# Rotary partners by a lane shuffle on VectorE instead of permutation matmuls, in a two-block transformer kernel

## The chip, the core and the metric

The kernel runs on one core of a Trainium2 chip. The metric is the device time of one execution, in microseconds (us). TensorE (PE in the profile, with PEld for its weight loads) multiplies matrices, VectorE (DVE), ScalarE (ACT) and GpSimd (POOL) work elementwise, and SyncE (SP) issues most of the DMAs. The engines run side by side and meet at semaphores. SBUF is the working memory, and PSUM has eight banks into which TensorE writes.

## The reference: two blocks over 256 tokens of width 1024

Everything is float32. The part that the change touches is the rotation of queries and keys in either block; the rest is named so that the stages can be followed.

```
# block 1: 8 heads of neighbourhood attention, 12 heads of dilated attention
h = rms_norm(x, norm_mix);  proj = h @ w_in
qd = partial_rotary(rms_norm(qd), pos)      # first 16 of each head's 64 channels
kd = partial_rotary(rms_norm(kd), pos)
    x1, x2 = xr[..., :8], xr[..., 8:16]
    rot = concat([x1*cos - x2*sin, x2*cos + x1*sin])
x = x + (sigmoid(gate_na) * (out_na @ w_branch_na)
         + sigmoid(gate_dil) * (out_dil @ w_branch_dil)) @ w_out
x = x + peer_ffn(rms_norm(x))               # 16384 experts, 8 heads x top 16
x = x + sigmoid(rms_norm(x) @ w_ple_gate) * (p @ w_ple)
# block 2: pooling branch and 4 differential-attention heads
q = apply_rope(q, cos, sin);  k = apply_rope(k, cos, sin)   # all 64 channels
    t1, t2 = split(t, 2)
    rope = concat([t1*cos - t2*sin, t1*sin + t2*cos])
x = x + mix @ w_o;  x = x + (silu(gate) * val) @ w_down;  out = rmsnorm(x)
```

## The kernel before

Activations stand with their channels on the 128 partitions and the 256 tokens along the free axis, so a chunk of 128 channels is a 128x256 tile and holds two heads of 64. All weights come in slots of 128x1024 (512 KB), loaded into `RAW` by SyncE. Each slot is split into a high part, rounded to fp32r by ScalarE (`split`, line 1101), and a low part, the difference, by VectorE or GpSimd (lines 1554 and 2273; `low_on_dve` says which). TensorE then makes three fp32r products for one weight block (`mm3`): high by high, high by low, low by high. There are three split buffers: slot n is split when TensorE has used slot n - 3, and loaded when the low part of slot n - 4 is made.

Each engine has its own program, written out in order. Generators set that order: `first_steps` for the first block's mixing part, `peer_steps` for the experts, `second_steps` for the second block's. Every step name stands in all five programs, and each program does its own part of it. Keys in `up` and `at` are semaphore counts; an engine waits in its own order only.

In the first block, step `ld n` computes chunk n of the 12 dilated query and key chunks (24 matmuls); `ev n` is ScalarE's part: copy the chunk with its gain into `qkd` (line 1144) and square it into one of four buffers `sqr` (line 1147). Step `dq i` rotates chunk i one step later. TensorE multiplies `qkd` by the constant 128x128 matrix `permd` in full float32, which exchanges channels 0 to 7 with 8 to 15 of each head with the sign (the result is the tile `rot` in PSUM), and `qk_sum` sums the squares of the chunk's two heads with two small matmuls per chunk. VectorE makes chunk x cos (line 1703), waits for TensorE's `rot`, multiplies it by sin (line 1708), and adds (line 1710). Steps `sc`, `tp` and `pv` between them are the scores, transposes and value products of the neighbourhood attention.

In the second block, `lin n` computes chunk n of 8; ScalarE copies it raw to `qk2` (`raw2`, line 1424); step `rp n` has TensorE multiply it by `permr`, which exchanges the 32-channel halves of each head, and VectorE makes the same three operations (lines 2143, 2147, 2149). The cos and sin tiles (`cosr`, `sinr`) already hold the norm's factor by token. Step `sc i` needs chunks 2i and 2i + 1 rotated; its scores are masked and their maxima taken by VectorE (lines 2156 to 2161), exponentiated by ScalarE (`exp`), combined by VectorE (`soft`).

The expert part has 128 slots `u` (projections; from slot 48 on each gives hidden values with a high and a low sum, added at line 2033) and 128 slots `v` (the way back). ScalarE applies gelu to slot u's values (line 1310), and VectorE multiplies in the gates (`gated_u`, line 1954), which frees the PSUM bank. Slot `v 0` begins the eight output sums in eight banks in the order 0, 1, 4, 5, 7, 6, 2, 3; the last of them needs the bank of slot u 127.

## Time and profile before

| | us |
|---|---|
| median of 3 runs | 1322.82 (1321.11 to 1323.88) |
| the profiled execution, its own time | 1317.93 |
| its span in the trace | 1315.8 |
| TensorE busy | 1302.9 |
| VectorE / ScalarE / GpSimd busy | 1013.6 / 827.2 / 520.3 |

The profiled execution is one run apart from the three timed ones. The span is what the trace covers; 2.1 us of the profiled execution's time lie around it. In a row of the timeline, the first number is the start in us from the span's start, the second how long the group lasts, then engine, line, operation, output<-inputs, shapes and the count of instructions; a bracket gives the idle time before it and what ended it. A matmul in full float32 stands as two records, an fp32r matmul as one. Matmuls are pipelined: each record's length is longer than the distance to the next one's start.

### The profile page before, as it was taken

The page shows a single profiled execution, that of the slowest core. Times are in us where ns is not written, and L with a number is a line of the kernel's source. Part 1 is how long each engine was busy: PE and PEld are TensorE (multiplying, and loading weights), DVE is VectorE, ACT ScalarE, POOL GpSimd, SP SyncE. Part 2 cuts the span into 40 slices and gives each one's busy share as a digit, 9 for nine tenths or more (in the row PEclk, how much of TensorE's full clock was granted, in tenths as well). Part 3 has the DMA queues.
Part 4 walks back from the last instruction along what each step waited for, and adds up shares of the span by engine and source line. Part 5 has one row for each costly group of instructions (what it writes and reads, how often), then busy time and mean ns, then how long its engine had stood idle before and what let it go on. Part 6 is the DMA issues. An engine that isn't in the chain of part 4 may idle for free.

```text
span 1315.8 us, 24814 instructions
## 1 busy us (share of the span) xinstructions
PE 1302.9 (99%) x9818; PEld 1257.0 (96%) x9818; DVE 1013.6 (77%) x1845; ACT 827.2 (63%) x1679; POOL 520.3 (40%) x252
## 2 busy tenths in 40 slices
PE   9999999999999999999999999999999999999998
PEld 9999899999999999999999999999999999999997
DVE  4483645859999888899978798998868845899943
ACT  5564646545455888888865566555566666666653
POOL 3745567678901000000024444324205463784442
PEclk9999999999999999999999999999999999999999
DMA  8433445445656554454579999999865543556552
GB/s 304 136 112 129 129 129 189 164 165 182 202 182 204 193 174 162 163 173 163 162 248 328 356 346 332 334 331 328 305 209 164 176 129 134 185 171 193 185 191 97
DMA packets 74299, 268.35 MB, mean 204 GB/s; under 512 B 8253, under 2 KB 8637, under 8 KB 74185
## 3 DMA queue, kind: packets, MB, share of 16 engines
q1 hardware_dynamic: 64968, 233.22, 52.5%
q0 software_dynamic: 9216, 33.56, 6.9%
q8 instruction: 78, 1.28, 0.4%
q14 instruction: 37, 0.30, 0.1%
HBM read 265.70 MB, written 1.05 MB: 203 GB/s over the span
## 4 chain that ended last, share of the span: by engine, by line
PE 83%; DVE 10%; POOL 4%; ACT 1%; DMA 1%; issue 1%; SPq 0%; DVEq 0%; ACTq 0%
PE PS L620 82%; POOL SPL L2273 2%; POOL HF L2332 1%; ACT SPL L1101 1%; DMA RAW<-in_ev 1%; DVE ixu L1844 1%; DVE Ssc L1838 1%; DVE ixu L1835 1%; PE PS L763 1%; DVE SPL L1554 1%; DMA RAW<-in_dense 1%; DVE bias L1633 0%; POOL HF L2330 0%; DVE top L1841 0%; DVE top L1832 0%
## 5 line engine op out<-in xcount | busy, mean ns | idle before, releaser
L1101 ACT ACTIVATE SPL<-RAW 128x1024 fp32r<-128x1024 f32 x429 | 453.7, 1059 | 363.0 <-PE PS L620 343.4
L620 PE MATMUL PS<-HS,SPL 128*128 128x224 f32 (+2 forms) x3968 | 531.4, 292 | 0.9 <-DVE SPL L1554 0.7
L620 PEld LDWEIGHTS PS<-HS,SPL 128*128 128x128 f32 x3968 | 502.5, 189 | 12.4 <-issue 1.7
L2273 POOL TENSOR_TENSOR SPL<-RAW,SPL 128x1024 fp32r<-128x1024 f32 x149 | 361.6, 2432 | 259.6 <-ACT SPL L1101 259.4
L1554 DVE TENSOR_TENSOR SPL<-RAW,SPL 128x1024 fp32r<-128x1024 f32 x280 | 345.3, 1235 | 142.6 <-ACT SPL L1101 140.3
L620 PE MATMUL PS<-asp,SPL 128*128 128x448 f32 (+1 forms) x2048 | 321.9, 319 | 1.6 <-DVE GB L1954 1.3
L620 PEld LDWEIGHTS PS<-asp,SPL 128*128 128x128 f32 x2048 | 307.5, 190 | 15.6 <-DVE GB L1954 1.6
L2303 POOL DMA_INDIRECT rows<-in_er,RS x16 | 27.9, 1743 | 281.4 <-PE PS L620 248.0
L620 PE MATMUL PS<-HXb,SPL 128*128 128x256 f32 x720 | 89.3, 284 | 0.7 <-issue 0.5
L620 PEld LDWEIGHTS PS<-HXb,SPL 128*128 128x128 f32 x720 | 87.4, 188 | 1.3 <-issue 1.0
L1317 ACT ACTIVATE oh<-oh,T3f 128x128 f32<-128x128 f32 x224 | 71.4, 404 | 0.0
L1934 DVE TENSOR_TENSOR oh<-CC,T3f 128x1024 f32<-128x1024 f32 x56 | 68.3, 1220 | 0.1
L2303 POOL DMA_INDIRECT urow<-in_er,RS x16 | 28.8, 1798 | 86.1 <-DVE RS L1946 59.1
L620 PE MATMUL PS<-actT,SPL 128*128 128x256 f32 x528 | 62.7, 281 | 0.0
L620 PEld LDWEIGHTS PS<-actT,SPL 128*128 128x128 f32 x528 | 62.6, 188 | 0.0
L620 PE MATMUL PS<-oh 128*128 128x128 f32 x448 | 60.1, 277 | 0.1
L620 PEld LDWEIGHTS PS<-oh 128*128 128x128 f32 x448 | 54.2, 191 | 2.0 <-ACT oh L1317 0.2
L1557 DVE TENSOR_TENSOR asp<-GB,asp 128x224 fp32r<-128x224 f32 x128 | 49.5, 387 | 1.7 <-ACT asp L1356 1.7
L1356 ACT ACTIVATE asp<-GB 128x224 fp32r<-128x224 f32 x128 | 47.8, 373 | 0.0
L2306 POOL DMA_INDIRECT rows<-in_ev,RS x16 | 28.7, 1796 | 47.3 <-DVE rows L2060 47.0
L620 PE MATMUL PS<-HXa,SPL 128*128 128x256 f32 x384 | 46.9, 282 | 0.5 <-POOL SPL L2273 0.5
L2306 POOL DMA_INDIRECT vrow<-in_ev,RS x16 | 26.8, 1676 | 50.3 <-DVE rows L2060 47.5
(296 smaller groups left out, 1525.3 us busy)
## 6 DMA issues: line engine op xcount, KB each, us to landing
RAW<-in_dense SPq DMA_DIRECT2D x176, 512.0 KB, 3.6
RAW<-in_eu SPq DMA_DIRECT2D x128, 512.0 KB, 3.5
RAW<-in_ev SPq DMA_DIRECT2D x128, 512.0 KB, 6.0
bias<-in_nab SPq DMA_DIRECT2D x2, 768.0 KB, 8.3
XT<-in_xT SPq DMA_DIRECT2D x4, 256.0 KB, 6.6
out_y<-HF SPq DMA_DIRECT2D x4, 256.0 KB, 2.2
c<-in_c SPq DMA_DIRECT2D x1, 960.0 KB, 8.9
c<-in_c SPq DMA_DIRECT2D x1, 512.0 KB, 4.7
```

The source lines that it names most:

```text
L620: return e.matmul(out, l, r, start=start, stop=stop, skip_group_check=skip)
L763: t = e.transpose(ps[:, j, a * 128:a * 128 + 128], probs_of(tag, i)[:, a * 256 * chunks + c * 256 + j * 128: a * 256 * chunks + c * 256 + ...
L1101: e.activation(spl(n)[0], raw(n), ACT.Copy).then_inc(*up("act_high", ("hi", n)))
L1317: q = e.activation(oh[m % 2][:, 1, j, :], oh[m % 2][:, 1, j, :], ACT.Copy, scale=T3f[:, 2, 4 * m + j:4 * m + j + 1])
L1356: e.activation(asp[i % 4][:, 0:W], GB[:, i, :], ACT.Copy).then_inc(*up("act_part", ("ahi", i)))
L1554: e.tensor_tensor(lo, raw(n), hi.bitcast(f32), ALU.subtract).then_inc(*up("dve_low", ("lo", n)))
L1557: return e.tensor_tensor(lo, x, hi.bitcast(f32), ALU.subtract).then_inc(*up("dve_part", *keys))
L1835: e.max_index(it[:, 0:8], vt[:, 0:8], v).then_inc(*up("dve_top", ("where1", k)))
L1934: e.tensor_tensor(oh[m % 2], con("iota").unsqueeze(1).unsqueeze(1).to_broadcast([128, 2, 4, 128]), T3f[:, 0:2, 4 * m:4 * m + 4].unsqueeze( ...
L2273: e.tensor_tensor(lo, raw(n), hi.bitcast(f32), ALU.subtract).then_inc(*up("pool_low", ("lo", n)))
L2303: e.indirect_dma_start(urow[j % 2], None, A["er"], rows_).then_inc(*up(f"urow{j % 2}", ("urow", j), by=16))
L2306: e.indirect_dma_start(vrow[j % 2], None, A["ev"].rearrange("a b c -> (a b) c"), rows_).then_inc(*up(f"vrow{j % 2}", ("vrow", j), by=16))
```

## The change

1. The matrices `permd` and `permr` and their 12 + 8 matmuls go. In step `dq`, VectorE's `stream_shuffle` moves the partitions of `qkd` in place within each group of 32 (`PARTNER_8`); the product with sin is then in SBUF, with the sign in the table. In step `rp`, the shuffle reads the chunk from PSUM and writes `qk2` (`PARTNER_16`), and ScalarE's `raw2` copies go. So that a half's partner lies within 32 partitions, the weights' columns of the second block's queries and keys are ordered anew by the host, the table of frequencies too.
2. `qk_sum` of two neighbouring chunks is done together, in the `dq` step of the odd one.
3. At the last `u` slot, ScalarE's `gelu(127)` and VectorE's `gated_u(127)` stand ahead of the split made in that slot. Before, they stood at the start of step `v 0`, behind it.

```diff
-for _n, _w in (("ident", 128), ("iota", 128), ("permd", 128), ("permr", 128), ("fold", TG)):
+for _n, _w in (("ident", 128), ("iota", 128), ("fold", TG)):
...
+PARTNER_8 = [*range(8, 16), *range(8), *range(16, 32)]
+PARTNER_16 = [*range(16, 32), *range(16)]
...
                 elif what == "dq":
-                    ps = take("scr1", "rot", i)
-                    w.wait_ge(*at("qksq", 8 + i))
-                    mm(ps[:, 0:256], con("permd"), qkd[:, i, :]).then_inc(*up("pe_rotate", ("full", "rot", i)))
-                    qk_sum(8 + i)
+                    if i % 2:
+                        qk_sum(7 + i)
+                        qk_sum(8 + i)
...
-                elif what == "rp":
-                    ps = take("scr3", "rp", i)
-                    w.wait_ge(*at("raw2", i))
-                    mm(ps[:, 0:256], con("permr"), qk2[:, i, :]).then_inc(*up("pe_rotate", ("full", "rp", i)))
...
                         if i > ROUTED:
                             gelu(i - 1)
+                    if i == NE - 1:
+                        gelu(i)
                     if i >= SUMS_FIRST:
                         split(cur[0] - 1 + NSPL)
...
                 elif what == "v":
-                    if i == 0:
-                        gelu(NE - 1)
...
-            def raw2(n):
-                w.wait_ge(*at("full", "qk2", n))
-                e.activation(qk2[:, n, :], psum("qk2", n)[:, 0:256], ACT.Copy).then_inc(*up("act_copy", ("raw2", n)))
...
-                    ps = psum("rot", i)[:, 0:256]
-                    w.wait_ge(*at("full", "rot", i))
-                    e.tensor_tensor(ps, ps, c1v["sind"], ALU.mult).then_inc(*up("dve_rotate", ("sined", i)))
+                    o = qkd[:, i, :]
+                    e.stream_shuffle(o, o, PARTNER_8).then_inc(*up("dve_rotate", ("swapped", i)))
+                    w.wait_ge(*at("swapped", i))
+                    e.tensor_tensor(o, o, c1v["sind"], ALU.mult).then_inc(*up("dve_rotate", ("sined", i)))
                     w.wait_ge(*at("sined", i))
-                    e.tensor_tensor(qkd[:, i, :], ps, rotm[i % 2],
-                                    ALU.add).then_inc(*up("dve_rotate", ("rotated", i), ("ev", "rot", i)))
+                    e.tensor_tensor(o, o, rotm[i % 2], ALU.add).then_inc(*up("dve_rotate", ("rotated", i)))
...
+                    if i == NE - 1:
+                        gated_u(i)
                     if i >= SUMS_FIRST:
                         split(cur[0] - 1 + NSPL)
                 elif what == "v":
-                    if i == 0:
-                        gated_u(NE - 1)
...
                 elif what == "rp":
-                    w.wait_ge(*at("raw2", i))
+                    o, ps = qk2[:, i, :], psum("qk2", i)[:, 0:256]
+                    w.wait_ge(*at("full", "qk2", i))
+                    e.stream_shuffle(o, ps, PARTNER_16).then_inc(*up("dve_rotate", ("swapped2", i)))
                     w.wait_ge(*at("turn2", 1))
-                    e.tensor_tensor(rm[i % 2], psum("qk2", i)[:, 0:256], cosr, ALU.mult).then_inc(
+                    e.tensor_tensor(rm[i % 2], ps, cosr, ALU.mult).then_inc(
                         *up("dve_rotate", ("cosed2", i), ("ev", "qk2", i)))
-                    ps = psum("rp", i)[:, 0:256]
-                    w.wait_ge(*at("full", "rp", i))
-                    e.tensor_tensor(ps, ps, sinr, ALU.mult).then_inc(*up("dve_rotate", ("sined2", i)))
+                    w.wait_ge(*at("swapped2", i))
+                    e.tensor_tensor(o, o, sinr, ALU.mult).then_inc(*up("dve_rotate", ("sined2", i)))
...
```

The next two pieces are TensorE's order in the first block, from the second chunk of the dilated queries on. `qkd,CC` is the matmul by `permd`, `CL,sqr` the sums of squares, `HS,SPL` the chunks' own matmuls, `qka` scores, `CC,prob` transposes and `probT,va` value products of the neighbourhood attention. First before, then changed:

```order
L620 MATMUL PS<-HS,SPL 128x256 x24
L620 MATMUL PS<-qkd,CC 128x256
L620 MATMUL PS<-CL,sqr 128x2 x2
L620 MATMUL PS<-HS,SPL 128x256 x24
L620 MATMUL PS<-qka 128x256 x4
L620 MATMUL PS<-qkd,CC 128x256
L620 MATMUL PS<-CL,sqr 128x2 x2
L620 MATMUL PS<-HS,SPL 128x256 x24
L763 MATMUL PS<-CC,prob 128x128 x8
L620 MATMUL PS<-qkd,CC 128x256
L620 MATMUL PS<-CL,sqr 128x2 x2
```

```order
L622 MATMUL PS<-HS,SPL 128x256 x48
L622 MATMUL PS<-qka 128x256 x4
L622 MATMUL PS<-CL,sqr 128x2 x4
L622 MATMUL PS<-HS,SPL 128x256 x24
L765 MATMUL PS<-CC,prob 128x128 x8
L622 MATMUL PS<-HS,SPL 128x256 x24
L622 MATMUL PS<-qka 128x256 x4
L622 MATMUL PS<-probT,va 64x256 x4
L622 MATMUL PS<-CL,sqr 128x2 x4
L622 MATMUL PS<-HS,SPL 128x256 x24
```

The matmuls by `permd` are gone, and the sums, two chunks at a time, stand only in the steps that also have scores or value products; every other step has transposes alone.

On VectorE in the second block, the rotations of the first chunks, behind the two products that put the norm's factor into `sinr` and `cosr`, and one low part of a split (`SPL<-RAW,SPL`); before, then changed:

```order
L2136 TENSOR_TENSOR cosr<-cosr,PS 128x256
L1554 TENSOR_TENSOR SPL<-RAW,SPL 128x1024
L2143 TENSOR_TENSOR rm<-PS,cosr 128x256
L2147 TENSOR_TENSOR PS<-PS,sinr 128x256
L2149 TENSOR_TENSOR qk<-PS,rm 128x256
L2143 TENSOR_TENSOR rm<-PS,cosr 128x256
L2147 TENSOR_TENSOR PS<-PS,sinr 128x256
L2149 TENSOR_TENSOR qk<-PS,rm 128x256
```

```order
L2126 TENSOR_TENSOR cosr<-cosr,PS 128x256
L1544 TENSOR_TENSOR SPL<-RAW,SPL 128x1024
L2133 STREAM_SHUFFLE qk<-PS 128x256
L2135 TENSOR_TENSOR rm<-PS,cosr 128x256
L2138 TENSOR_TENSOR qk<-qk,sinr 128x256
L2140 TENSOR_TENSOR qk<-qk,rm 128x256
L2133 STREAM_SHUFFLE qk<-PS 128x256
L2135 TENSOR_TENSOR rm<-PS,cosr 128x256
L2138 TENSOR_TENSOR qk<-qk,sinr 128x256
```

Each rotation has one instruction more, and the product with sin reads SBUF instead of TensorE's result in PSUM.

On ScalarE at the passage from the `u` to the `v` slots (`rows<-PS` is the copy of the low sum at slot u 127, `PS<-PS 128x224` the gelu, `SPL<-RAW` a split, `asp<-GB` the high part of gated values for the `v` slots); before, then changed:

```order
L1334 ACTIVATE rows<-PS 128x224
L1310 ACTIVATE PS<-PS 128x224
L1101 ACTIVATE SPL<-RAW 128x1024
L1356 ACTIVATE asp<-GB 128x224
L1310 ACTIVATE PS<-PS 128x224
L1101 ACTIVATE SPL<-RAW 128x1024
```

```order
L1331 ACTIVATE rows<-PS 128x224
L1307 ACTIVATE PS<-PS 128x224 x2
L1098 ACTIVATE SPL<-RAW 128x1024
L1355 ACTIVATE asp<-GB 128x224
L1098 ACTIVATE SPL<-RAW 128x1024
```

The gelu of slot 127 moves ahead of one split and one copy; on VectorE, `gated_u(127)` moves in the same way ahead of the low part of that split and of `asp`.

## Rows read from the trace of the kernel before

**Rows 1.** The page: busy time (share) by engine, and the granted clock by slice

```profile
PE 1302.9 (99%) x9818; PEld 1257.0 (96%) x9818; DVE 1013.6 (77%) x1845; ACT 827.2 (63%) x1679; POOL 520.3 (40%) x252
...
PEclk9999999999999999999999999999999999999999
```

**Rows 2.** Groups by shape, TensorE: count, busy us, mean ns, idle before

```profile
L620 PE MATMUL PS<-qkd,CC 128*128 128x256 f32 x24 | 7.7, 401 | 0.0
...
L620 PE MATMUL PS<-qk,CC 128*128 128x256 f32 x16 | 4.9, 398 | 0.0
```

**Rows 3.** Timeline, TensorE, 74.5 to 80.1 us: start, length, instruction, count

```profile
74.52 0.70 PE L620 MATMUL PS<-qkd,CC 128*128 128x256 f32 x2
75.06 0.50 PE L620 MATMUL PS<-CL,sqr 128*128 128x2 f32 x4
75.42 3.05 PE L620 MATMUL PS<-HS,SPL 128*128 128x256 f32 x24
...
79.18 0.60 PE L620 MATMUL PS<-qkd,CC 128*128 128x256 f32 x2
79.61 0.50 PE L620 MATMUL PS<-CL,sqr 128*128 128x2 f32 x4
```

**Rows 4.** Timeline, TensorE, 18.9 to 23.3 us

```profile
18.99 0.95 PE L620 MATMUL PS<-CL,sqr 128*128 128x2 f32 x8
19.80 3.07 PE L620 MATMUL PS<-HS,SPL 128*128 128x256 f32 x24
```

**Rows 5.** Busy time of VectorE in two stretches: length, busy, clock, DMA, GB/s

```profile
55.00:113.00 58.00, 39.33 (x92) 1.00 0.34 110
1029.00:1070.00 41.00, 32.82 (x71) 1.00 0.47 151
```

**Rows 6.** Timeline, TensorE, 1035.1 to 1051.6 us

```profile
1038.13 1.02 PE L620 MATMUL PS<-qk,CC 128*128 128x256 f32 x4
1039.08 0.60 PE L620 MATMUL PS<-CL,RS 1*128 1x1 f32 x4
1039.61 3.14 PE L620 MATMUL PS<-HXb,SPL 128*128 128x256 f32 x24
...
1045.98 0.93 PE L620 MATMUL PS<-qk 64*128 64x128 f32 x8
...
1050.36 0.93 PE L620 MATMUL PS<-qk 64*128 64x128 f32 x8
```

**Rows 7.** Timeline, VectorE, 1035 to 1050 us

```profile
1035.96 1.75 DVE L1566 RECIPROCAL RS<-RS 128x256 f32<-128x256 f32 x1 [1.28 <-ACT RS L1121]
1037.75 1.23 DVE L1554 TENSOR_TENSOR SPL<-RAW,SPL 128x1024 fp32r<-128x1024 f32 x1
...
1041.15 0.42 DVE L2143 TENSOR_TENSOR rm<-PS,cosr 128x256 f32<-128x256 f32 x1
...
1042.29 0.41 DVE L2143 TENSOR_TENSOR rm<-PS,cosr 128x256 f32<-128x256 f32 x1
...
1047.02 1.02 DVE L2156 SCALAR_TENSOR_TENSOR sb<-PS,c 128x384 f32<-128x384 f32 x2 [2.39 <-PE PS L620]
...
1049.00 0.42 DVE L2143 TENSOR_TENSOR rm<-PS,cosr 128x256 f32<-128x256 f32 x1
```

**Rows 8.** Timeline, all engines, 672.3 to 677 us

```profile
673.04 2.36 PE L620 MATMUL PS<-asp,SPL 128*128 128x448 f32 x14
...
673.77 1.05 ACT L1101 ACTIVATE SPL<-RAW 128x1024 fp32r<-128x1024 f32 x1
673.82 0.39 DVE L2033 TENSOR_TENSOR PS<-PS,rows 128x224 f32<-128x224 f32 x1
...
675.00 0.35 ACT L1310 ACTIVATE PS<-PS 128x224 f32<-128x224 f32 x1
...
676.29 0.38 DVE L1954 TENSOR_TENSOR GB<-GB,PS 128x224 f32<-128x224 f32 x1
...
676.73 0.47 PE L620 MATMUL PS<-asp,SPL 128*128 128x448 f32 x1 [1.32 <-DVE GB L1954]
```

More of the change, by code:

```diff
@@ L259 @@
     scalar_tensor_tensor = tensor_copy = tensor_reduce = reciprocal = memset = dma_start = op
-    max = max_index = match_replace = indirect_dma_start = op
+    max = max_index = match_replace = indirect_dma_start = stream_shuffle = op
 class Once:
@@ L1444, in act_program @@
                 if what == "pair":
-                    raw2(0)
-                    raw2(1)
                     std(3, ("bank7", "o"))
@@ L1452, in act_program @@
                     step()
-                    raw2(i)
                 elif what == "rT":
@@ L2140, in dve_program @@
                 elif what == "rp":
-                    w.wait_ge(*at("raw2", i))
+                    o, ps = qk2[:, i, :], psum("qk2", i)[:, 0:256]
+                    w.wait_ge(*at("full", "qk2", i))
+                    e.stream_shuffle(o, ps, PARTNER_16).then_inc(*up("dve_rotate", ("swapped2", i)))
                     w.wait_ge(*at("turn2", 1))
-                    e.tensor_tensor(rm[i % 2], psum("qk2", i)[:, 0:256], cosr, ALU.mult).then_inc(
+                    e.tensor_tensor(rm[i % 2], ps, cosr, ALU.mult).then_inc(
                         *up("dve_rotate", ("cosed2", i), ("ev", "qk2", i)))
-                    ps = psum("rp", i)[:, 0:256]
-                    w.wait_ge(*at("full", "rp", i))
-                    e.tensor_tensor(ps, ps, sinr, ALU.mult).then_inc(*up("dve_rotate", ("sined2", i)))
+                    w.wait_ge(*at("swapped2", i))
+                    e.tensor_tensor(o, o, sinr, ALU.mult).then_inc(*up("dve_rotate", ("sined2", i)))
                     w.wait_ge(*at("sined2", i))
-                    e.tensor_tensor(qk2[:, i, :], ps, rm[i % 2],
-                                    ALU.add).then_inc(*up("dve_rotate", ("rotated2", i), ("ev", "rp", i)))
+                    e.tensor_tensor(o, o, rm[i % 2], ALU.add).then_inc(*up("dve_rotate", ("rotated2", i)))
                 elif what == "sc":
@@ L2403, in _constants @@
     put(c0, C0, "iota", np.arange(128)[None, :])
-    m = np.zeros((128, 128), np.float32)
-    r = np.zeros((128, 128), np.float32)
-    for b in (0, 64):
-        for j in range(8):
-            m[b + 8 + j, b + j] = -1.0
-            m[b + j, b + 8 + j] = 1.0
-        for j in range(32):
-            r[b + 32 + j, b + j] = -1.0
-            r[b + j, b + 32 + j] = 1.0
-    put(c0, C0, "permd", m)
-    put(c0, C0, "permr", r)
     c1 = np.zeros((128, NC1), np.float32)
@@ L2434, in _constants @@
             cosd[b + j] = np.cos(ang[j % 8])
-            sind[b + j] = np.sin(ang[j % 8])
+            sind[b + j] = np.sin(ang[j % 8]) * (1.0 if j >= 8 else -1.0)
     put(c1, C1, "cosd", cosd)
@@ L2457, in _layout @@
     up = f("w_up_2")[0]
+    halves = np.arange(64).reshape(2, 2, 16).transpose(1, 0, 2).reshape(64)
+    in2 = f("w_in_2")[0].copy()
+    in2[:, 512:1536] = in2[:, 512:1536].reshape(1024, 16, 64)[:, :, halves].reshape(1024, 1024)
     o = [j for k in range(22) for j in (k, k + 22)]
@@ L2462, in _layout @@
         _blocks(f("w_out")[0]), _blocks(f("peer_w_query")[0]), _blocks(f("w_ple")[0]),
-        _blocks(f("w_ple_gate")[0]), _blocks(f("w_in_2")[0], [4, 8, 5, 9, 6, 10, 7, 11, *range(12, 16), *range(4)], (8, 10, 12, 14)), _blocks(f("w_o_2")[0]), _blocks(up, o),
+        _blocks(f("w_ple_gate")[0]), _blocks(in2, [4, 8, 5, 9, 6, 10, 7, 11, *range(12, 16), *range(4)], (8, 10, 12, 14)), _blocks(f("w_o_2")[0]), _blocks(up, o),
         _blocks(f("w_down_2")[0], blocks=[22 * n + kk for n, kk in down_blocks()])])
@@ L2490, in _layout @@
                     ("o128", np.full((128, 1), 1.0 / 128)), ("one", np.ones((128, 1))),
-                    ("invf", inv.astype(np.float32)[p % 32][:, None])):
+                    ("invf", (inv[halves[p % 64] % 32] * np.where(halves[p % 64] < 32, -1, 1)).astype(np.float32)[:, None])):
         put(name, v)
```

## The prediction, as it was put on record

> **What bounds the kernel now.** I read the page's busy times first. TensorE is busy 1302.9 of 1315.8 us, 99%, VectorE 77%, ScalarE 63%, and TensorE's granted clock is in its top tenth in every slice, which is the upper of its two levels, 2.4 GHz [rows 1]. So a microsecond of TensorE's queue is a microsecond of the span, unless taking it out makes TensorE wait for something else. Next I read the groups by shape, to find what the change removes there, then the timeline of TensorE at those places, then VectorE's beside it, because VectorE must now do TensorE's share. The last view is the timeline of all engines at 673 to 677 us, one of TensorE's few long stops: 1.32 us, ended by VectorE's gate product for slot 127 [rows 8].
>
> **Part 1, the twelve matmuls by `permd`.** The groups show 24 records (two for each full float32 matmul) with a mean of 401 ns and 7.7 us busy, and 16 records with 4.9 us for `permr` [rows 2]. Matmuls overlap, so I don't sum lengths but distances between starts. A matmul by `permd` starts at 79.18 and what follows it at 79.61: 0.43 us. The one at 74.52 has 0.54 us to 75.06 [rows 3]; it stands behind a product over 64 channels, and I take its extra 0.1 as the price of that passage, which the sums now pay in its place. So 12 x 0.43 = 5.2 us, all in TensorE's queue. The busy time of the group, 7.7, is the upper bound.
>
> The Trainium skill says the same of such a sum in "Trainium Kernel Development and Optimization", section Performance Expectations: busy time of matmuls is a bad measure since they are pipelined. By busy time, parts 1 and 2 would give 12.6 us; by starts they give 8.7. The rows side with the starts, since 0.60 us of length ends well after the next group's start at 79.61 [rows 3].
>
> **The sums in one stretch.** A stretch of one chunk lasts 0.36 us to the next group's start (75.06 to 75.42) [rows 3], one of two chunks 0.81 (18.99 to 19.80) [rows 4]. Two single ones are 0.72, so a join costs 0.09 there, and saves one passage back into fp32r matmuls, which no row prices by itself. Six joins: I take 0. Bounds: 0.5 us worse (6 x 0.09) and 0.6 better (6 x 0.1, the size of the other passage).
>
> **Who pays for part 1.** VectorE gets 12 shuffles of 128x256. The trace has no shuffle. The nearest rows are its 128x256 products, 0.42 us each [rows 7]; the most expensive 128x256 operation it has is the reciprocal, 1.75 us [rows 7]; the lower bound is nothing. I take 0.42, since a shuffle only moves elements. VectorE is busy 39.3 of 58.0 us in this stretch [rows 5]; with 12 x 0.42 = 5.0 it is 44.4 of 52.8, so there is room. The shuffled chunks are needed only for the dilated scores, behind the stretch, so nothing in TensorE's queue waits for them there. VectorE also loses its wait for TensorE's `rot`. What could wait is TensorE for a PSUM bank of chunk n - 3, which VectorE frees in its first operation of step `dq`, ahead of the shuffle. I cost that at nothing; if the cover were gone, the price is counted in the rivals.
>
> The Trainium skill gives a price: in "VectorE: DVE Perf Modes", section The perf-mode tier table, a shuffle of 2048 float32 elements per partition takes about 2400 ns against 2293 for a `tensor_tensor`. By that ratio, an estimate, a shuffle here would be 0.44 us and the sum would stay as it is. No row of this trace shows it.
>
> **Part 2, the eight matmuls by `permr`.** 8 x 0.43 = 3.5 us from TensorE's queue (at 1038.13 two of them and what lies to the next start are 0.95, that is 0.47 each [rows 6]). Here the cover is thin. Two places:
>
> The fourth slot of the stretch (`lin 3`). TensorE starts it at 1039.61. Without the two matmuls ahead, and with 0.53 for the small ones between 1039.08 and 1039.61, it would be ready at 1038.13 + 0.53 = 1038.66 [rows 6]. But its low part is made by VectorE in 1037.75 to 1038.98, right behind the reciprocal, and that does not move [rows 7]. A start at about 1039.05: 0.39 us of the gain is a new wait.
>
> Second scores (`sc 1`). They need chunks 2 and 3 rotated. A rotation takes 1.14 us now (1041.15 to 1042.29, three instructions [rows 7]), so 1.52 with a fourth of the same step. The first three end at 1041.15 + 4.56 = 1045.71. The first scores, at 1045.98 now, come three matmuls earlier less the wait: 1045.98 - 1.30 + 0.39 = 1045.07 [rows 6]. VectorE begins masking 1.04 us behind them (1045.98 to 1047.02 [rows 6, 7]), at 1046.11, so the rotations are just done. Masking and maxima take 1.98 us to the next rotation (1047.02 to 1049.00 [rows 7]), so chunk 3 is rotated at 1046.11 + 1.98 + 1.52 = 1049.6. TensorE would reach `sc 1` at 1050.36 - 1.73 + 0.39 = 1049.0 [rows 6]. So it waits another 0.6. Later chunks come in pairs and have more time between; I take no more there. VectorE's sum agrees that it fits: 32.8 busy of 41.0, and 36.2 of 37.5 with eight shuffles [rows 5].
>
> Part 2 brings 3.5 - 0.4 - 0.6 = 2.5 us. The eight ScalarE copies that go lie beside TensorE's work and bring nothing themselves.
>
> **Part 3, the last slot's gates.** TensorE stops for 1.32 us until 676.73, for the bank that `gated_u(127)` frees at 676.29 + 0.38. In front of it stood gelu at 675.00 behind a split of 1.05 us on ScalarE [rows 8]. Moved, gelu can start when VectorE's sum is done, 673.82 + 0.39 = 674.2, ends at 674.6, and the product at about 675.0. TensorE wants the bank at 676.73 - 1.32 = 675.41, so the whole 1.3 us goes. What is late instead is the split, by about 0.8 us: ScalarE 674.6 to 675.65, VectorE's low part until about 676.9. It belongs to `v 2`. TensorE needs 2.36 us for 14 of a slot's 16 matmuls [rows 8], 2.7 for a slot, so `v 2` begins at 673.04 + 5.4 = 678.4, with 1.5 us to spare. The load that waits for this low part (four slots on) is issued 0.8 us later; it has two slots more. I cost both at nothing.
>
> **Sum.** 5.2 + 2.5 + 1.3 = 9.0 us off the profiled execution's 1317.93: 1308.9. That execution ran 4.9 us below the median of the timed runs, 1322.82, so the time to be measured is 1322.82 - 9.0 = 1313.8 us.
>
> **Rivals.**
> Everything hidden (the two new waits don't come, or the joined sums gain): 5.2 + 3.5 + 1.3 = 10.0, 1312.8 us. For it: VectorE's waits for TensorE's `permr` results also go. Against it: the low part at 1038.98 is not touched by the change.
>
> A shuffle costs two instructions of 0.42. A rotation in the second block then takes 1.9 us, the first three end at 1046.85, chunk 3 is done at 1046.85 + 1.98 + 1.9 = 1050.7, and TensorE waits 1.7 instead of 0.6: part 2 brings 1.4, the sum is 7.9, 1314.9 us. In the first block, 39.3 + 12 x 0.84 = 49.4 of 52.8 still fits. The Trainium skill speaks for an extra instruction: "Vector Engine (DVE) Microarchitecture Reference", section 3.8, has the permutation loaded by an instruction of its own before the shuffle. No row here shows it.
>
> The passage to the `v` slots gains nothing, because the late split or its load is met by TensorE after all: 7.7, 1315.1 us. Against it the 1.5 us to spare.
>
> VectorE becomes the bound, and the kernel is slower: a shuffle priced like the reciprocal, 1.75 us. VectorE has (52.8 - 39.3) / 12 = 1.1 us of room per shuffle in the first block and (37.5 - 32.8) / 8 = 0.6 in the second [rows 5]. Above these each shuffle's excess is TensorE's wait: 12 x 0.65 + 8 x 1.15 = 17.0, less 10.0 gained: 7 us slower, 1329.8. It turns from gain to loss at 12(p - 1.1) + 8(p - 0.6) = 10.0, p = 1.4 us. For it: nothing in the trace bounds a shuffle below that. Against it: the reciprocal computes, the copies and products of the same size are all near 0.42.
>
> The change does not do what it says (TensorE waits for squares of two chunks at each joined stretch, and about as much as was taken): near 1322. Against it: the later chunk's squares were already waited for at this place.
>
> **How the numbers follow.** Forecast 0.52; everything hidden 0.15; two instructions 0.13; passage gains nothing 0.08; no change 0.05; VectorE the bound 0.07. About 0.2% (2.6 us) is what a measurement of this kernel tells from no change. Faster 0.88, same 0.05, slower 0.07. The first four cases lie between 1312.8 and 1315.1; medians of three runs scatter by a good microsecond on either side (1321.11 to 1323.88 here), and the bounds of the joined sums are half a microsecond. The range is 1311.3 to 1317.0.
>
> **What would show it.** In the changed profile: no matmuls by constants between 59 and 112 us, and score steps about 0.86 us closer per two chunks; TensorE's groups before 1100 us start about 7.7 us plus the passage's 1.3 earlier; a wait of about 0.4 us at the fourth slot of the second block ended by VectorE's low part, and about 0.6 us at the second scores ended by VectorE's rotation; no stop of 1.3 us at the first `v` slot; shuffles of 0.42 us. The prediction is wrong if shuffles last over a microsecond, if TensorE waits in the first block, or if the second block gives back more than 2 us.

## The result, and the profile after

The changed kernel took 1328.82 us (median of 5 runs, 1328.46 to 1332.7), the kernel before 1321.39 us beside it (1319.84 to 1323.88): a ratio of 1.0071, 95% interval [1.0053, 1.0089]. It is 7 us slower, where 9 us faster was forecast. Here and below, medians and ratios are of the executions in the fast state alone; e1 and e6 had one slow execution each (3259 and 2046 us). The profiled execution of the changed kernel took 1328.58 us, its span is 1326.5 us against 1315.8.

The page of the changed kernel, busy time by engine, against [rows 1]:

```profile
PE 1299.8 (98%) x9778; PEld 1253.8 (95%) x9778; DVE 1042.6 (79%) x1885; ACT 824.9 (62%) x1671; POOL 521.2 (39%) x252
```

TensorE has its 40 fewer records, but is idle for 1326.5 - 1299.8 = 26.7 us instead of 12.9. VectorE is busy 29 us longer, though 20 shuffles at the forecast 0.42 us make 8.4. The waits of TensorE say where the idle time is. Columns: who waited, for whose result, us in total, times, longest:

```profile
PE PS L622 <- DVE qk L2140: 5.8, 2, 4.4
PE PS L622 <- DVE rotm L1693: 5.3, 3, 2.7
PE PS L622 <- DVE sb L2146: 2.2, 1, 2.2
```

13.3 us in six stops, all ended by VectorE, in the two attention blocks; none of these rows was there before. The groups by shape of VectorE in those blocks say that it is not the shuffle. Columns behind the bar: busy time in us and mean length in ns, then idle time before. First from 55 to 113 us, then from 1025 to 1092:

```profile
L1623 DVE TENSOR_SCALAR prob<-prob,statb 128x256 f32<-128x256 f32 x16 | 15.3, 1000 | 0.3
L1699 DVE TENSOR_TENSOR qkd<-qkd,c 128x256 f32<-128x256 f32 x11 | 6.5, 595 | 0.4
L1697 DVE STREAM_SHUFFLE qkd<-qkd 128x256 f32<-128x256 f32 x12 | 5.3, 443 | 0.0
```

```profile
L2138 DVE TENSOR_TENSOR qk<-qk,sinr 128x256 f32<-128x256 f32 x8 | 6.5, 814 | 0.0
L2165 DVE SCALAR_TENSOR_TENSOR sb<-sb,sst 128x128 f32<-128x128 f32 x4 | 5.6, 1400 | 0.1
L2140 DVE TENSOR_TENSOR qk<-qk,rm 128x256 f32<-128x256 f32 x8 | 5.5, 682 | 0.3
L2161 DVE SCALAR_TENSOR_TENSOR sst<-sst,SM 128x2 f32<-128x2 f32 x4 | 5.0, 1253 | 0.1
L2133 DVE STREAM_SHUFFLE qk<-PS 128x256 f32<-128x256 f32 x8 | 3.6, 445 | 0.0
```

The shuffles take 0.44 us, close to the 0.42 I took. The products and sums beside them, 0.42 us when they read PSUM, have means of 0.6 to 0.8. Three more groups are long that the change did not touch: the scaling of probabilities (`L1623`) and the two steps in which `soft` combines the second block's probabilities (`L2161`, `L2165`). The timeline of VectorE ahead of the longest stop shows what the means hide:

```profile
1042.63 0.45 DVE L2133 STREAM_SHUFFLE qk<-PS 128x256 f32<-128x256 f32 x1
1042.97 0.41 DVE L2135 TENSOR_TENSOR rm<-PS,cosr 128x256 f32<-128x256 f32 x1
1043.30 1.96 DVE L2138 TENSOR_TENSOR qk<-qk,sinr 128x256 f32<-128x256 f32 x1
1045.30 2.48 DVE L2140 TENSOR_TENSOR qk<-qk,rm 128x256 f32<-128x256 f32 x1
...
1048.38 2.06 DVE L2138 TENSOR_TENSOR qk<-qk,sinr 128x256 f32<-128x256 f32 x1
1050.47 0.42 DVE L2140 TENSOR_TENSOR qk<-qk,rm 128x256 f32<-128x256 f32 x1
```

GpSimd beside it, which makes low parts of weight slots (two in the first row):

```profile
1041.84 5.67 POOL L2263 TENSOR_TENSOR SPL<-RAW,SPL 128x1024 fp32r<-128x1024 f32 x2 [13.21 <-ACT SPL L1098]
1047.82 2.34 POOL L2263 TENSOR_TENSOR SPL<-RAW,SPL 128x1024 fp32r<-128x1024 f32 x1 [0.32 <-ACT SPL L1098]
```

And TensorE, with the stop of 4.37 us for two chunks that, at the forecast 1.52 us each, would have been rotated at 1042.63 + 3.04 = 1045.67:

```profile
1040.60 5.99 PE L622 MATMUL PS<-HXb,SPL 128*128 128x256 f32 x48 [0.30 <-DVE SPL L1544]
1050.95 1.35 PE L622 MATMUL PS<-qk 64*128 64x128 f32 x8 [4.37 <-DVE qk L2140]
1052.23 4.24 PE L622 MATMUL PS<-HXb,SPL 128*128 128x256 f32 x24
```

The reader is to compare ends. The product of 1048.38 ends at 1050.44, the low part of 1047.82 at 1050.16; the two of 1043.30 and 1045.30 end at 1045.26 and 1047.78, the two low parts at 1044.98 and 1047.50. Each ends 0.28 us behind a low part. The shuffle and the product `rm<-PS,cosr` start in the same stretch and take 0.45 and 0.41. Slow are those whose inputs lie both in SBUF. Before the change, product and sum read the partner from PSUM.

The first block shows it on an instruction that the change did not touch, the scaling of probabilities from SBUF to SBUF (two in each row):

```profile
70.11 2.80 DVE L1623 TENSOR_SCALAR prob<-prob,statb 128x256 f32<-128x256 f32 x2
...
73.02 2.64 DVE L1623 TENSOR_SCALAR prob<-prob,statb 128x256 f32<-128x256 f32 x2
```

```profile
70.39 4.87 POOL L2263 TENSOR_TENSOR SPL<-RAW,SPL 128x1024 fp32r<-128x1024 f32 x2 [3.06 <-ACT SPL L1098]
```

Before, two scalings of this block waited like this, and it was there to be read. The first fence is the scalings' group from 55 to 113 us (a mean of 605 ns; their median is 352) and the pair at 71 us, the second is GpSimd beside it:

```profile
L1633 DVE TENSOR_SCALAR prob<-prob,statb 128x256 f32<-128x256 f32 x16 | 9.0, 605 | 0.3
...
71.03 2.76 DVE L1633 TENSOR_SCALAR prob<-prob,statb 128x256 f32<-128x256 f32 x2
```

```profile
70.99 2.38 POOL L2273 TENSOR_TENSOR SPL<-RAW,SPL 128x1024 fp32r<-128x1024 f32 x1 [3.77 <-ACT SPL L1101]
```

After, five scalings of this block wait, and three products of the rotation. The second block's later stops, of 1.5 and 2.2 us, stand behind instructions that the change did not touch and that waited too, here those ahead of the stop of 2.2 (GpSimd made two low parts from 1072.70 to 1077.43):

```profile
1072.82 2.29 DVE L2161 SCALAR_TENSOR_TENSOR sst<-sst,SM 128x2 f32<-128x2 f32 x1
1075.14 2.83 DVE L2165 SCALAR_TENSOR_TENSOR sb<-sb,sst 128x128 f32<-128x128 f32 x2
```

Counted over both blocks, six products and sums waited, 8.7 us above their usual lengths, and nine untouched scalings and combining steps, 18.7 us; before, three of these waited, 6.1 us. The likely reason is that VectorE's and TensorE's changed steps shifted VectorE's order against GpSimd's; no run isolates that. The waiting is booked as busy time. VectorE's stretches, to be read against [rows 5], with 44.4 and 36.2 us forecast:

```profile
55.00:113.00 58.00, 51.36 (x114) 0.97 0.33 109
1029.00:1070.00 41.00, 38.55 (x73) 0.96 0.45 141
```

The Trainium skill states this in "SBUF — State Buffer", section SBUF: two separate sides: the port pair that GpSimd and VectorE share is "an exclusive lock, not a bandwidth split", needed by a VectorE instruction in a two-port mode or with two SBUF inputs, and whoever starts first holds it for the whole instruction. The trace agrees: 1.96 to 2.48 us in place of 0.42, with ends tied to the low part's.

Last, TensorE's clock, in stretches of the changed kernel. Columns: stretch, length, busy and records, granted clock, DMA share, GB/s:

```profile
1047.00:1051.00 4.00, 0.05 (x2) 1.00 0.65 220
1050.90:1055.00 4.10, 4.05 (x22) 0.58 0.41 134
1055.00:1060.00 5.00, 5.00 (x43) 1.00 0.01 2
```

Behind the stop of 4.4 us the granted clock is at the lower level, 1.2 GHz, for 3.4 us; so it is behind the stops of 2.75 us (at 92 us) and 2.2 us (at 1079), and not behind those of 2.0 and 1.5. In this stretch 24 matmuls take 4.24 us instead of 3.13 and the eight scores ahead of them 1.35 instead of 0.93: 1.5 us. Taken for each of the three stretches, an estimate, that is 4.5.

The books: 8.7 us of work out of TensorE's queue (the forecast's figure), 13.8 of idle time in (26.7 - 12.9, in which the 1.3 us that part 3 takes out is counted), 4.5 for the clock: 13.8 + 4.5 - 8.7 = 9.6 us of the span's 10.7. The last 1.1 us I can't place.

### The profile page after: what moved, and what is told of

Read it like the earlier page. It is cut to its first block, busy times and chain, and to the rows that moved or that the text cites. A ratio compares the mean times of both kernels' runs of the same rounds, so it can differ in the third digit from the quotient of the medians.

```text
span 1326.5 us, 24765 instructions
## 1 busy us (share of the span) xinstructions
PE 1299.8 (98%) x9778; PEld 1253.8 (95%) x9778; DVE 1042.6 (79%) x1885; ACT 824.9 (62%) x1671; POOL 521.2 (39%) x252
## 4 chain that ended last, share of the span: by engine, by line
PE 82%; DVE 14%; DMA 1%; ACT 1%; issue 1%; SPq 0%; POOL 0%; DVEq 0%; ACTq 0%
PE PS L622 81%; DMA RAW<-in_ev 1%; DVE ixu L1834 1%; DVE Ssc L1828 1%; DVE ixu L1825 1%; DVE prob L1623 1%; ACT SPL L1098 1%; DMA RAW<-in_dense 1%; DVE SPL L1544 1%; DVE sb L2165 0%; DVE bias L1623 0%; DVE top L1831 0%; DVE top L1822 0%; DVE HF L1561 0%; DVE qpc L1874 0%
## 5 line engine op out<-in xcount | busy, mean ns | idle before, releaser
L622 PEld LDWEIGHTS PS<-HXa,SPL 128*128 128x128 f32 x384 | 45.9, 188 | 0.7 <-issue 0.6
```

Source lines behind the costliest of these rows:

```text
L622: return e.matmul(out, l, r, start=start, stop=stop, skip_group_check=skip)
```

## The experiments

Theory P: VectorE instructions with two SBUF inputs, or scaling from SBUF to SBUF, wait for the end of a running low part on GpSimd, and this costs the 16 us between forecast and result. Rival A: the fourth instruction of each rotation is the cost (VectorE has too little room), wherever operands lie. In the recorded expectations of e1, e5, e7 and e8 rival A is called theory W; e7's theory A and the rivals A of e9, e11 and e12 are others, told where they are answered. "The kernel before" of each ratio ran beside it on the same chip. The cuts of code leave out waits and semaphore updates.

### The partner in PSUM (e1)

```diff
-e.stream_shuffle(o, ps, PARTNER_16)
-e.tensor_tensor(rm[i % 2], ps, cosr, ALU.mult)
-e.tensor_tensor(o, o, sinr, ALU.mult)
-e.tensor_tensor(o, o, rm[i % 2], ALU.add)
+e.tensor_tensor(rm[i % 2], ps, cosr, ALU.mult)
+e.stream_shuffle(ps, ps, PARTNER_16)
+e.tensor_tensor(ps, ps, sinr, ALU.mult)
+e.tensor_tensor(o, ps, rm[i % 2], ALU.add)   # block 1 likewise, its shuffle from qkd to ps
```

> The changed kernel with one difference: in both blocks the cos product is made first, the shuffle then writes its result into the chunk's own PSUM tile, and the product with sin and the sum read that PSUM tile and one SBUF tile. Same count of instructions on every engine as the changed kernel. Theory P (a VectorE instruction with both tensor inputs in SBUF cannot run beside a GpSimd split and waits for its end): products and sums stay at 0.42 us, TensorE's stops of 4.4 us in the second block and of 0.5 us at 111 us go, and the time is below the kernel before, 1311 to 1316 us. Theory W (VectorE simply has one instruction too many per chunk and falls behind): it stays slower than before, 1326 to 1330 us.

Measured 1326.97 us, 1.0056 [1.004, 1.0072]: as a way to repair the kernel it failed. It missed theory P's range and lies in that of rival A, so its time does not speak for P. Its timeline does, on the length of single instructions. VectorE, then GpSimd:

```profile
1047.02 0.43 DVE L2140 TENSOR_TENSOR PS<-PS,sinr 128x256 f32<-128x256 f32 x1
1047.48 0.42 DVE L2142 TENSOR_TENSOR qk<-PS,rm 128x256 f32<-128x256 f32 x1
...
1048.74 0.43 DVE L2140 TENSOR_TENSOR PS<-PS,sinr 128x256 f32<-128x256 f32 x1
1049.21 0.42 DVE L2142 TENSOR_TENSOR qk<-PS,rm 128x256 f32<-128x256 f32 x1
```

```profile
1045.31 5.49 POOL L2266 TENSOR_TENSOR SPL<-RAW,SPL 128x1024 fp32r<-128x1024 f32 x2 [13.22 <-ACT SPL L1098]
```

With one input in PSUM, product and sum pass beside the low parts at 0.42 us. The stop of 4.4 us went down to 0.8. But the chunk's bank now comes free only behind the sum, and the untouched instructions wait as before (five scalings, and in the second block two each of the combining steps, 1.7 to 2.5 us); TensorE's waits are other ones of the same size:

```profile
PE PS L622 <- DVE qkd L1702: 5.4, 3, 3.1
PE PS L622 <- DVE qk L2142: 3.8, 3, 2.0
```

### Each part alone (e2, e3, e4)

e2 is the kernel before with part 3 (`gelu` and `gated_u` of the last slot ahead of the split), e3 with part 1 and the joined sums, e4 with part 2, each exactly as in the change's diff.

> The kernel before with part 3 alone (the last slot's gelu and gate product ahead of the split). Theory from the prediction: the stop of 1.32 us at the first v slot goes and the late split costs nothing: 1.3 us faster than before, about 1320.1 us. Rival: the late split or its load is met later: no difference.

> The kernel before with parts 1 and the joined sums alone (shuffle in the first block, both inputs of the product in SBUF). The trace of the changed kernel shows there stops of 1.99, 2.75 and 0.54 us and one stretch of 3.4 us at the lower clock (about 1.5 us lost) against 5.1 us removed. Theory P and W both: 1 to 3 us slower than before. If the alignment of VectorE's prob products with GpSimd's splits is a matter of chance, it may also be 0 to 5 us faster; the trace tells which.

> The kernel before with part 2 alone (shuffle in the second block). The trace of the changed kernel shows there new stops of 4.4, 0.3, 0.5, 1.5, 2.2 and 0.2 us, and two stretches of 3.4 us at the lower clock (about 1.5 us each), 12 us in all against 3.5 us removed: 7 to 9 us slower than before, 1328 to 1331 us. If the second block is not the main cause: within 2 us of before.

Measured, with the kernel before at 1318.88: part 3 alone 1316.41 us, 0.9983 [0.9975, 0.9992]; part 1 alone 1322.82 us, 1.0023 [1.001, 1.0037]; part 2 alone 1327.78 us, 1.0065 [1.0052, 1.0078]. The product of the three is 1.0071, the ratio of the whole. Part 2 carries most of the loss; its trace has the stops of the changed kernel (4.4, 1.4, 2.2 us). Part 1 alone spread from 1316.34 to 1327.26 over 12 runs: how many scalings wait for a low part is not fixed (e10 below has the changed kernel's first block, and its trace has four such scalings where the changed kernel's has five), which may be why.

### GpSimd's low parts cut short (e5, e6)

```diff
-e.tensor_tensor(lo, raw(n), hi.bitcast(f32), ALU.subtract)
+k = 16 if n >= 4 and (n < SLOT0["wout"] or n >= SLOT0["w_in2"] + 2 * NE) else 1024
+e.tensor_tensor(lo[:, 0:k], raw(n)[:, 0:k], hi[:, 0:k].bitcast(f32), ALU.subtract)
```

> The changed kernel, with GpSimd's low part of each split in the first block's stages before the output projection and in all of the second block made on 16 columns instead of 1024; the rest of the low part is left out (stale values stay there). VectorE's programme is untouched. Theory P (what costs is that VectorE's instructions with two SBUF inputs, and its fast SBUF to SBUF scalings, and GpSimd's splits exclude each other): every VectorE instruction keeps its short length, TensorE's new stops go, and what the change removed from TensorE shows: 8 to 10 us below the kernel before. Theory W (VectorE has too much to do in its order, even undisturbed): TensorE still waits for it, and the time stays above the kernel before minus 3 us.

> The kernel before with the same cut of GpSimd's low parts (16 of 1024 columns, the rest left out). It says what the same removal brings where TensorE hardly waits. Both theories: within 2 us below the kernel before. If it were far faster, the other run would say nothing on the change.

In both the rest of each such low part is left out. Measured: the changed kernel with short low parts 1308.68 us, 0.9913 [0.9896, 0.993]; the kernel before with the same cut 1317.3 us, 0.999 [0.998, 1.0]. VectorE's program was not touched, and its groups in the second block went back to one step each:

```profile
L2140 DVE TENSOR_TENSOR qk<-qk,rm 128x256 f32<-128x256 f32 x8 | 3.4, 424 | 0.3
L2138 DVE TENSOR_TENSOR qk<-qk,sinr 128x256 f32<-128x256 f32 x8 | 3.3, 415 | 0.0
```

This is the experiment that decides. With next to nothing to meet on GpSimd, the change brings 1317.3 - 1308.68 = 8.6 us; the forecast's sum was 9.0. By the ratios it is 0.8%, 10 us, and the two intervals leave more than 2 us on either side, so the agreement with 9.0 is no closer than that. Rival A would have left it slow. The two new waits of part 2 are there too, where the prediction put them, 0.30 us at the fourth slot and 0.72 at the second scores (forecast: 0.4 and 0.6):

```profile
1034.29 5.98 PE L622 MATMUL PS<-HXb,SPL 128*128 128x256 f32 x48 [0.30 <-DVE SPL L1544]
1040.20 0.93 PE L622 MATMUL PS<-qk 64*128 64x128 f32 x8
1041.06 3.13 PE L622 MATMUL PS<-HXb,SPL 128*128 128x256 f32 x24
1044.92 0.93 PE L622 MATMUL PS<-qk 64*128 64x128 f32 x8 [0.72 <-DVE qk L2140]
```

### No shuffles, and the scalings on ScalarE (e7, e8)

Both start from e1. e7 leaves the 20 shuffles out, so chunks are rotated with themselves as partner; e8 lets ScalarE scale the neighbourhood probabilities (`activation(..., ACT.Copy, scale=b[:, 4 + a:5 + a])` in place of `tensor_scalar`).

> The kernel with the rotation's operands in PSUM, without the 20 shuffles (the partners are left out, so the rotation is not computed): VectorE has the same three instructions per chunk as before, TensorE has no permutation matmuls. Theory W (the added instruction): the stops go and it is 8 to 10 us faster than before. Theory A (alignment: with TensorE's steps shorter, VectorE's scalings of the probabilities and its softmax sums meet GpSimd's splits, shuffle or not): some stops stay, and it is less than 6 us faster.

> The kernel with the rotation's operands in PSUM, and ScalarE instead of VectorE scales the probabilities of the neighbourhood attention (16 instructions of 128x256). Theory P/A: the stops of 1.6, 3.1 and 0.7 us in the first block and the two stretches at the lower clock that followed there (about 10 us together with the 6.8 us stretch) go, the second block's stay: 1318 to 1321 us, that is as before. Theory W: VectorE has 16 instructions fewer there, so the same; but then the stops are shorter in proportion to 6 us of work, and not gone. Rival: ScalarE, with 6 us more in that stretch, becomes late with its splits: TensorE waits for ScalarE or GpSimd there, and it is no faster than 1325.

Measured: e7 1315.24 us, 0.997 [0.996, 0.998]; e8 1321.66 us, 1.002 [1.0006, 1.0033]. e7 is 4.0 us below the kernel before, short of the 8 to 10 that rival A asked for and inside the range of theory A (what counts is how VectorE's instructions fall against GpSimd's low parts). Against e1's 1.0056, 20 instructions of 0.43 us less are worth 0.9%, about 11 us, more than their own 8.6 us of VectorE: the shuffle's share in e1 is large. But e7's scalings met no low part (mean 351 ns, where e1 has 969), and nothing but the 20 missing instructions in VectorE's order brought that about. So e7 does not separate room from encounters; e5 does. e8, just above its range, takes the scalings out of reach and gets two thirds of e1's loss back; its block 2 still stops, for 0.8, 1.0, 1.9 and 1.8 us.

### Low parts in four pieces (e9, e11), and a filler for the clock (e10)

```diff
-e.tensor_tensor(lo, raw(n), hi.bitcast(f32), ALU.subtract)
+for c in range(0, 1024, 256):   # in the slots of e5's condition
+    e.tensor_tensor(lo[:, c:c + 256], raw(n)[:, c:c + 256], hi[:, c:c + 256].bitcast(f32), ALU.subtract)
```

e11 is the kernel before with part 3 and the same pieces. e10 is the changed kernel with nine extra matmuls ahead of the first scores of block 2: `mm(bank(7)[:, 256:512], con("ident"), CC[:, 0:256])`.

> The changed kernel with GpSimd's low parts of the two blocks each done by four instructions of 256 columns in place of one of 1024; the whole computation is done. Theory P (a product or sum of VectorE with both inputs in SBUF waits for the end of the GpSimd instruction that runs, and for that one alone): one piece takes (2.34 - 0.24)/4 + 0.24 = 0.77 us by the rows of the full and of the 16-column low part, so no VectorE instruction of the turns is longer than about 0.42 + 0.77 = 1.2 us instead of 2.0 to 2.5, the stops of TensorE of 4.4, 2.7, 2.2 and 2.0 us shrink to under 1.5 us each, no stretch at the lower clock follows, and the time is 1309 to 1317 us. Rival A (VectorE is held for as long as GpSimd has work, piece behind piece, or the cost is the total of GpSimd's work): the four pieces take 3.1 us together, the waits grow to 3 us, and the time is 1328 to 1336 us.

> The kernel before with the third part of the change alone (last slot's gates ahead of a split) and with GpSimd's low parts of the two blocks in four pieces of 256 columns each. It tells how much of what the pieces bring is there without the lane shuffle. Theory P: in the kernel before only the scalings of probabilities met a running split (twice, 2.4 us each, and behind no stop of TensorE worth more than 0.6 us), so the pieces change little against that kernel with the third part alone (ratio 0.9983): 0.997 to 0.999. Rival A (GpSimd's pieces cost more than they free, or bring the same here as with the shuffle): below 0.996 or above 1.0.

> The changed kernel with nine extra fp32 matmuls 128x128 by 128x256 (0.43 us each, 3.8 us together), whose result nobody reads, in TensorE's order just ahead of the first scores of block 2, where it stood still for 4.4 us. Theory C (the stretch at 1.2 GHz behind that stop comes of the stop, and costs 1.4 to 1.6 us by the 24 matmuls that took 4.2 us instead of 3.0): the granted clock stays at full from 1047 to 1060 us, the 24 matmuls behind the scores take about 3.0 us, the time is 1.0 to 1.8 us below that of the changed kernel, 1327.0 to 1327.9 us, a ratio to the kernel before of about 1.0058 to 1.0064 instead of 1.0071. Rival D (the clock falls for another reason): the stretch at the lower clock stays where it was, and the time is 1328.5 to 1329.5 us.

Measured: e9 1321.62 us, 1.0024 [1.0013, 1.0036]; e11 1323.48 us, 1.0031 [1.0019, 1.0044]; e10 1327.91 us, 1.0077 [1.0057, 1.0098]. e9 missed its range by 5 us, and the control tells why: pieces cost 0.5% in the kernel before, too (1.0031 against 0.9983 for part 3 alone). So e11 missed its range as well, on its rival's side: GpSimd's pieces cost more than they free. In the feed-forward layers TensorE now waits for low parts (in e9, by GpSimd):

```profile
PE PS L622 <- POOL SPL L2266: 4.7, 8, 1.2
```

The filler did in the trace what theory C expects. Its ratio missed the range (1.0058 to 1.0064), and no more can be said of its time, since six runs spread over 8 us (1324.67 to 1332.98). With TensorE kept at work, what follows the first scores runs at the upper level:

```profile
1042.71 4.05 PE L622 MATMUL PS<-CC 128*128 128x256 f32 x18
1047.25 0.93 PE L622 MATMUL PS<-qk 64*128 64x128 f32 x8 [0.49 <-DVE qk L2144]
1048.11 3.13 PE L622 MATMUL PS<-HXb,SPL 128*128 128x256 f32 x24
```

Yet in that trace a later stop of 2.2 us, behind which the clock had fallen before, was not followed by the lower level, and one of 2.0 us at 79 us was. So the stop's length alone doesn't tell. Nor does the lower level need a stop: in seven traces (e1, e3, e4, e5, e8, e11 and e13) it came between 119 and 129 us, for 3.4 us (6.8 in e1), in or just behind a run of twelve matmuls over 12 rows (`rsT,bsel`, 2.85 us), with TensorE busy without a gap from 113 us on. In e11 (stretch, length, busy and records, granted clock, DMA share, GB/s):

```profile
113.00:119.90 6.90, 6.90 (x59) 1.00 0.45 152
...
124.80:128.20 3.40, 3.40 (x19) 0.51 0.64 219
```

The same matmuls stand in all sixteen traces, and in the other nine the clock stayed up there.

### Pieces in the two attention blocks alone (e12, e13, e14)

e12 and e14 are e9 and e11 with the condition narrowed to `n < SLOT0["wout"] or 0 <= n - SLOT0["w_in2"] - 2 * NE < 16`; e13 is e1 with the same.

> The changed kernel with GpSimd's low parts in four pieces of 256 columns in the two attention blocks alone (from the fourth slot to the first block's projections, and the 16 slots of block 2's), not in the feed-forward layers behind, where the same pieces made TensorE wait six times 0.57 us and 1.2 us for a low part; the whole computation is done. Theory P: those waits of about 5 us go and all else stays as it was with pieces everywhere (ratio 1.0024), so 0.998 to 0.9995, 1316 to 1318 us, level with the kernel before or a little below it. Rival A (what the pieces freed was freed behind the blocks, or the cost of the pieces falls in the blocks): 1.001 to 1.004.

> As the run with pieces in the blocks alone, with the partner written to PSUM, as in the first experiment, so that products and sums have one input in SBUF and wait for no split; the whole computation is done. Theory P: the 13 products and sums that still waited 0.3 to 0.6 us each do not wait any more, and the two longest stops left in block 2 (2.0 and 1.1 us) shrink; 0.995 to 0.9985, 1312 to 1317 us, below both kernels. Rival B (with the partner in PSUM the bank of a chunk comes free only after the sum, some 1.3 us later, and TensorE waits for banks instead): no better than with the partner in SBUF, 0.999 to 1.002.

> The kernel before with the third part alone and the pieces in the two blocks alone. Theory P: the kernel before loses next to nothing to running splits, so the pieces bring it nothing there and cost little: 0.9975 to 0.999, the same as the third part alone (0.9983). If it comes out below 0.997, the pieces are a gain of their own and what they gave the changed kernel is no measure of the shuffle's loss.

Measured: e12 1314.24 us, 0.9967 [0.9954, 0.998]; e13 1315.54 us, 0.9977 [0.9964, 0.999]; e14 1317.28 us, 0.9987 [0.9976, 0.9997]. e12 came out below its range (0.998 to 0.9995), against its rival, by which the pieces' cost falls in the blocks. The whole change with its low parts in pieces is below the kernel before and 1.0% below the change as it was made. e12's VectorE at the place of the 4.4 us stop, and GpSimd:

```profile
1037.80 0.99 DVE L2138 TENSOR_TENSOR qk<-qk,sinr 128x256 f32<-128x256 f32 x1
1038.82 0.85 DVE L2140 TENSOR_TENSOR qk<-qk,rm 128x256 f32<-128x256 f32 x1
```

```profile
1036.34 3.05 POOL L2265 TENSOR_TENSOR SPL<-RAW,SPL 128x256 fp32r<-128x256 f32 x3 [12.55 <-ACT SPL L1098]
```

A product now waits for one piece (0.99 - 0.42 = 0.57 us), not for the rest of the slot: the exclusion is by instruction, not for as long as GpSimd has work, which was e9's rival. The shorter waits remain, and with them stops of 1.1 and 2.0 us at the two scores, where e5 has one of 0.7; behind that of 2.0 us the clock is at the lower level for 3.4 us (1049.8 to 1053.2). The scores make 2.3 of the 5.7 us between the spans of e12 and e5 (1313.3 and 1307.6), the stop at 751 us told below another 1.5. e13 did not better this: with the partner in PSUM the products wait for no piece and block 2's stops are shorter in sum (0.8, 1.0 and 0.9 us against 1.1, 2.0 and 0.7), but the bank comes free later, and block 1 stops for 0.2, 0.6 and 0.7 us where e12 has one stop of 0.2.

Part of e12's gain is given back far behind. TensorE stops for 2.9 us at 751 us, where the kernel before stopped for 0.3, and what it waits for is a load that ScalarE got late:

```profile
748.83 1.06 ACT L1098 ACTIVATE SPL<-RAW 128x1024 fp32r<-128x1024 f32 x1 [6.07 <-DMA RAW<-in_ev]
```

This stop has 1.5 us in e5, 4.7 in e8 and is missing in e14; why, I have not found out.

The control says that the pieces by themselves bring nothing (0.9987 against 0.9983 for part 3 alone). Of the versions that compute everything, e12 is the fastest; its interval overlaps with that of part 3 alone, so that it beats the latter is likely, not shown. Against e14, its own control on the same chip, it is 3.0 us faster: ten of e12's twelve executions lie below 1315.9 us, two of e14's twelve. That is what the shuffle brought with the pieces in place.

## Why the prediction was wrong

**What TensorE's queue loses.** Right. In e5's trace TensorE is busy 1294.8 us, in e6's 1302.3: 7.5 less, although e5's has a stretch of 3.4 us at the lower clock that e6's lacks (about 1.5 us by the one above), so some 9 against the 8.7 forecast. In time the whole change brought 8.6 us there, against 9.0.

**The joined sums.** A stretch of two chunks takes 0.91 us (63.41 to 64.32 in the changed kernel) where I had 0.81. Six times 0.1 is inside the bound of 0.5 that I gave. No run isolates it.

**The shuffle's own price.** Right: 0.44 us against 0.42. The estimate from the Trainium skill's table, also 0.44, came out as well, though the table has its 2400 ns in the bf16 column and gives float32 the same tier without a time. The extra instruction of the rival is there too, and takes 0.01 us.

**Who pays for part 1, and the 1.52 us of a rotation in part 2.** This step failed. I priced a rotation as "a fourth of the same step", 0.42 each, and looked only at how many instructions there are. The wait for GpSimd's low parts stood nowhere in the sum. The shuffle moved the operands of the two instructions behind it: product and sum went from PSUM to SBUF. In the first 8 us of part 2's rotations that made 1.96, 2.48 and 2.06 us out of three steps of 0.42: 5.2 us. By the forecast's prices the two chunks had 0.9 us to spare (rotated at 1045.67, TensorE ready at 1050.95 - 4.37 = 1046.58); the rest became the stop of 4.4 us.

Two terms that I had put at nothing came with it: TensorE's wait for the bank that the cos product frees (`rotm`), three stops, 5.3 us, in the first block; and the later chunks of the second block, "I take no more there", with stops of 1.5 and 2.2 us. These stand behind waits of instructions that the change did not touch, and which make most of the waiting; with the operands back in PSUM (e1, e13) little or nothing was gained. Two of the prediction's own signs of being wrong came true, waits in the first block and a second block that gives back more than 2 us.

The room by busy time was misleading twice. It counted VectorE's free time, of which there was enough (e5), and not what GpSimd was doing at those moments; and a wait for the port is told as busy time, 51.4 of 58 us in the first block, where 44.4 was forecast, so the group's mean of 605 ns for scalings with a median of 352 stood in the trace before and would have given it away.

**The stops and the clock.** I had no term for a stop's sequel. The three longest brought stretches at 1.2 GHz, 1.5 us each.

**Part 3.** Right in mechanism: 1.3 us forecast, 2.5 measured (1318.88 to 1316.41), with an interval of 0.08 to 0.25%, about 1.1 to 3.3 us, that holds the forecast; in the traces of the changed kernel and of e2 the first `v` slot has no stop. Between the two traces lie 2.7 us, 1.3 of them the stop. Another 0.8 us lie ahead of 20 us, where both kernels run the same steps, so they are scatter between two executions and no gain of part 3.

**The rivals.** "VectorE becomes the bound" gave 1329.8 us, near what came out, and for the wrong reason: it let the shuffle cost 1.75 us. The one I should have had was a wait of VectorE for GpSimd, whose low parts, about 2.4 us each, stood in both stretches.

## What to carry to other kernels

When a change adds VectorE instructions, shifts their order or moves an operand from PSUM to SBUF, price it by what GpSimd runs beside it, not by the instruction's length: here 0.42 us became up to 2.5. Moving the operand back alone did not repair it, since other instructions waited too. Look in the trace before for instructions of one group that are several times as long as their median, and lay GpSimd's timeline beside them. If GpSimd's instructions must run there, cut them into pieces where TensorE does not wait for them, and only there: 1.0% here, and it would have cost 0.5% elsewhere. The shuffle itself is worth having once that is done: 3.0 us here (e12 against e14).

## What the runs showed of the hardware

A `stream_shuffle` of 128x256 float32 takes 0.44 us from SBUF or PSUM, and its mask is loaded by an instruction of 0.01 us. It was never seen slowed by a low part, even with input and output in SBUF; the scaling from SBUF to SBUF was (0.35 us became 2.3 to 2.5), which I had not expected of an instruction with one large input, and so was a `scalar_tensor_tensor` of only 128x2 (0.22 us became 2.3).

GpSimd seems to be held as well: the first of the two low parts at 1041.84 began beside VectorE's own low part (two SBUF inputs, 1.22 us from 1041.49), and the two took 5.67 us, where the next took 2.34 by itself; at the same place in e1 the two took 5.49. No run was made for this.
